# The step and gate-rank columns of a projection: from narrow moving operands to weights in four column groups

## What is computed

```python
z, xbc, dt_raw, q, k, v, g_out, gk_low = jnp.split(h @ p['w_in'], offsets, axis=-1)
gf = jax.nn.log_sigmoid((gk_low @ p['gk_up_f'] + p['gk_bias_f']).astype(f32)) / GLA_GATE_NORM
gb = jax.nn.log_sigmoid((gk_low @ p['gk_up_b'] + p['gk_bias_b']).astype(f32)) / GLA_GATE_NORM
'dt_f': jax.nn.softplus((dt_raw + p['dt_bias_f']).astype(f32)),
'dt_b': jax.nn.softplus((dt_raw + p['dt_bias_b']).astype(f32)),
```

## Time and profile before

| what | value |
|---|---|
| median of three runs | 2600.0 us |
| time of the profiled execution | 2598.53 us |
| its span, first to last instruction | 2596.5 us |
| TensorE busy over the span | 2285.3 us (88%) |
| mean granted TensorE clock over the span | 0.913 of 2.4 GHz |
| span from the first feature product to the last step's small products | 64.17 to 666.31 us |
| TensorE busy in it | 587.5 of 602.14 us, granted clock 0.90 |
| VectorE, ScalarE busy in it | 199.3 us, 129.4 us |

### The profile page before, as it was taken

The page is one execution under the profiler, slowest core; times in us unless marked ns, Lnnn a source line. Parts: engine busy times, 40 slices in busy tenths (PEclk is TensorE's granted clock), DMA queues, the critical chain, the costliest instruction groups (busy, mean ns, idle before and its releaser), DMA issues. The chain is left out here.

```text
span 2596.5 us, 37174 instructions
## 1 busy us (share of the span) xinstructions
PE 2285.3 (88%) x12243; PEld 1813.3 (70%) x12243; DVE 1604.0 (62%) x2000; ACT 1136.2 (44%) x1469; POOL 565.7 (22%) x535
## 2 busy tenths in 40 slices
PE   3999999999689997599999804999999999999990
PEld 1777777766467776588888703887778787878770
DVE  1233333323353443777777353999999999999993
ACT  0122221222255553223233103777777777777772
POOL 1000000000000000144344143333333333333332
PEclk7988898988889998599999857999999999999995
DMA  7123322332276664588787261647897868989967
GB/s 278 58 95 108 108 77 94 108 108 92 101 267 232 237 243 170 196 289 262 253 271 234 65 222 43 201 126 230 281 318 238 293 213 285 351 259 347 340 226 275
DMA packets 207806, 531.79 MB, mean 205 GB/s; under 512 B 14624, under 2 KB 47803, under 8 KB 204635
## 3 DMA queue, kind: packets, MB, share of 16 engines
q1 hardware_dynamic: 180587, 434.68, 46.4%
q0 software_dynamic: 23664, 83.18, 13.1%
q10 hardware_dynamic: 3456, 12.58, 1.3%
HBM read 400.77 MB, written 129.62 MB: 204 GB/s over the span
## 5 line engine op out<-in xcount | busy, mean ns | idle before, releaser
L547 PE MATMUL pf<-hT,w_in_sb 128*128 128x256 f32 x1440 | 331.5, 395 | 1.1 <-DVE hT L628 1.1
L547 PEld LDWEIGHTS pf<-hT,w_in_sb 128*128 128x128 f32 x1440 | 286.5, 200 | 43.5 <-DVE hT L628 1.5
L2019 ACT ACTIVATE w_hi_e<-w_gates 128x2048 fp32r (+1 forms) x103 | 197.5, 1919 | 234.4 <-issue 103.4
L2145 DVE TENSOR_TENSOR w_lo_e<-w_gates,w_hi_e 128x2048 fp32r<-128x2048 f32 x103 | 236.3, 2295 | 33.4 <-ACT w_hi_e L2019 33.4
L2145 DVE TENSOR_TENSOR w_lo_e<-w_ups,w_hi_e 128x2048 fp32r<-128x2048 f32 x102 | 233.5, 2289 | 36.0 <-ACT w_hi_e L2019 35.9
L2145 DVE TENSOR_TENSOR w_lo_e<-w_downs,w_hi_e 128x2048 fp32r<-128x2048 f32 x100 | 228.3, 2283 | 0.0
L2019 ACT ACTIVATE w_hi_e<-w_ups 128x2048 fp32r (+1 forms) x102 | 195.2, 1913 | 26.3 <-PE pd_e L2092 24.6
L2019 ACT ACTIVATE w_hi_e<-w_downs 128x2048 fp32r x100 | 191.1, 1911 | 0.9
L2092 PE MATMUL pg_e<-w_hi_e,x_hi_e 128*128 128x512 f32 x408 | 167.1, 410 | 7.1 <-DVE w_lo_e L2145 7.1
L1997 POOL DMA_INDIRECT x_mid<-yb_e,to_e x50 | 126.9, 2538 | 190.7 <-DVE yb_e L2189 188.7
L2092 PE MATMUL pd_e<-w_hi_e,h_hi_e 128*128 128x512 f32 x400 | 162.1, 405 | 0.0
(11 more groups left out here) (363 smaller groups left out, 4669.1 us busy)
## 6 DMA issues: line engine op xcount, KB each, us to landing
w_gates<-in_w_gate_dram SPq DMA_DIRECT2D x32, 2048.0 KB, 11.6
w_ups<-in_w_up_dram SPq DMA_DIRECT2D x32, 2048.0 KB
w_downs<-in_w_down_dram SPq DMA_DIRECT2D x32, 2048.0 KB
tok_rec<-tm SPq DMA_DIRECT2D x9, 1936.0 KB, 7.2
rec_s<-tok_rec SPq DMA_DIRECT2D x18, 968.0 KB, 6.0
w_mod_half<-in_w_mod_dram SPq DMA_DIRECT2D x16, 1024.0 KB, 6.4
abc_m<-a_rows SPq DMA_DIRECT2D x16, 1024.0 KB, 4.9
qk_rec<-qk_s SPq DMA_DIRECT2D x16, 768.0 KB, 3.2
```

The source lines that it names most:

```text
L547: mm = pe.matmul(pf[n % 2][:, f, :], w[:, k, c0:c0 + P], h[:, k, :], start=(k == 0), stop=(k == KT - 1))
L2019: act.activation(w_hi[:, s % 3:s % 3 + 1, :], raw(part, half, place), ACT.Copy).then_inc(hi_done, 1)
L2145: dve.tensor_tensor(w_lo[:, s % 3:s % 3 + 1, :], raw(part, half, place), w_hi[:, s % 3:s % 3 + 1, :].bitcast(F32), ALU.subtract).then_inc( ...
```

## The change

The step and gate-rank columns become the weights: `w_small` holds 8 step columns, 16 gate-rank columns and 8 columns of zeros, and the eight products of a step go to four groups of 32 partitions of `psm` in turn (feature tiles 0 and 4 to the first, and so on), with all 256 tokens as the moving operand. What comes out is already in feature order, in four partial sums. VectorE copies it once to `quarters` [128 x 256] and adds column 24 of the identity, which makes row 24 a row of ones. The gate product takes `quarters` as weights against a `gk_up` matrix of 128 rows that has the 16 rows of the gates in each of the four groups and the biases in row 24, so that the product adds up the four partial sums. The steps come by two products against `sel_dt` (128 x 16), and VectorE copies these to `small_sb`. The two transposes and the two bias products are gone. The loads of the small matrices are 12 where they were 6.

```diff
-            sp.dma_start(w_small[:, :, 16:32], ...[:, :, O_GK:]).then_inc(w_in_loaded, 16)
+            sp.dma_start(w_small[:, :, SH:SH + RANK], ...[:, :, O_GK:]).then_inc(w_in_loaded, 16)
...
-        small_sb = sb("small_sb", [P, 2, 32])
-        gkT = sb("gkT", [RANK + 1, 2, P])
-        up = sb("gk_up", [RANK + 1, 2 * GQK])
-        dtb = sb("dt_bias", [1, 2 * SH])
+        small_sb = sb("small_sb", [P, 2, 2 * SH])
+        quarters = sb("quarters", [P, GRP])
+        up, sel_dt = sb("gk_up", [P, 2 * GQK]), sb("sel_dt", [P, 2 * SH])
...
+            sp.wait_ge(const_done, 3)
+            for d, n in enumerate(("f", "b")):
+                for j in range(4):
+                    sp.dma_start(up[32 * j + SH:32 * j + SH + RANK, GQK * d:GQK * (d + 1)], A[f"gk_up_{n}"][0]).then_inc(small_loaded, 16)
+                sp.dma_start(up[ONE:ONE + 1, GQK * d:GQK * (d + 1)], A[f"gk_bias_{n}"]).then_inc(small_loaded, 16)
+            sp.wait_ge(wsm_done, 3)
+            for d, n in enumerate(("f", "b")):
+                sp.dma_start(sel_dt[ONE:ONE + 1, SH * d:SH * (d + 1)], A[f"dt_bias_{n}"]).then_inc(small_loaded, 16)
...
+                    act.wait_ge(dt_done, it + 1)
+                    act.activation(soft[s][:, 512:528], small_sb[:, s, :], ACT.Abs).then_inc(abs_done, 1)
...
-            pool.memset(gkT[:, :, :], 1.0).then_inc(const_done, 1)
-            pool.wait_ge(const_done, 2)
+            pool.memset(up[:, :], 0.0).then_inc(const_done, 1)
+            pool.memset(w_small[:, :, ONE:32], 0.0).then_inc(const_done, 1)
+            pool.wait_ge(const_done, 3)
...
-                for s in range(2):
-                    for k in range(KT):
-                        pe.matmul(psm[:, s * 32:s * 32 + 32], h[:, k, s * P:(s + 1) * P], w_small[:, k, :],
-                                  start=(k == 0), stop=False)
-                    mm = pe.matmul(psm[:, s * 32:s * 32 + 16], C["ones"][0:1, :], dtb[0:1, :], start=False, stop=True)
+                for k in range(KT):
+                    j = k % 4
+                    mm = pe.matmul(psm[32 * j:32 * j + 32, 0:GRP], w_small[:, k, :], h[:, k, :], start=(k < 4), stop=(k >= 4))
                 mm.then_inc(small_ps, 1)
...
+                if is_ctx:
+                    pe.wait_ge(small_loaded, 16 * 12)
                 for s in range(2):
-                    mm = pe.transpose(psm[0:RANK, 128 + s * P:256 + s * P], small_sb[:, s, 16:32], ident[:, :])
-                mm.then_inc(gk_ps, 1)
-                pe.wait_ge(gk_done, it + 1)
+                    mm = pe.matmul(psm[:, GRP + 2 * SH * s:GRP + 2 * SH * (s + 1)], quarters[:, s * P:(s + 1) * P], sel_dt[:, :], start=True, stop=True)
+                mm.then_inc(dt_ps, 1)
                 pe.wait_ge(tok_done, it * 2 + 2)
                 for s in range(2):
-                    pe.matmul(pz[s][:, :], gkT[:, s, :], up[:, :], start=True, stop=True).then_inc(g_ps, 1)
+                    pe.matmul(pz[s][:, :], quarters[:, s * P:(s + 1) * P], up[:, :], start=True, stop=True).then_inc(g_ps, 1)
...
+            for d in range(2):
+                dve.tensor_reduce(sel_dt[:, SH * d:SH * (d + 1)], ident[:, :].rearrange("p (j c) -> p c j", j=4)[:, 0:SH, :], AX,
+                                  ALU.add).then_inc(wsm_done, 1)
...
-                dve.tensor_copy(small_sb[:, :, :], psm[:, 0:64].rearrange("p (s c) -> p s c", s=2)).then_inc(small_done, 1)
+                dve.tensor_scalar(quarters[:, :], psm[:, 0:GRP], ident[:, ONE:ONE + 1], None, ALU.add).then_inc(small_done, 1)
...
-                dve.wait_ge(gk_ps, it + 1)
-                dve.tensor_copy(gkT[0:RANK, :, :], psm[0:RANK, 128:384].rearrange("p (s c) -> p s c", s=2)).then_inc(gk_done, 1)
+                dve.wait_ge(dt_ps, it + 1)
+                dve.tensor_copy(small_sb[:, :, :], psm[:, GRP:GRP + 4 * SH].rearrange("p (s c) -> p s c", s=2)).then_inc(dt_done, 1)
```

More of the change, by code:

```diff
@@ L261, in _ @@
                 sp.dma_start(w_in_sb[:, k, :], A["w_in"][0][k * P:(k + 1) * P, O_XBC:O_G]).then_inc(w_in_loaded, 16)
-            sp.dma_start(w_small[:, :, 16:32], A["w_in"][0].rearrange("(k p) c -> p k c", p=P)[:, :, O_GK:]).then_inc(w_in_loaded, 16)
+            sp.dma_start(w_small[:, :, SH:SH + RANK], A["w_in"][0].rearrange("(k p) c -> p k c", p=P)[:, :, O_GK:]).then_inc(w_in_loaded, 16)
         @block.gpsimd
@@ L320, in projection @@
     NF = 10
+    ONE = SH + RANK
     col = [i * P for i in range(6)] + [o - O_XBC for o in (O_Q, O_Q + P, O_K, O_K + P)]
@@ L359, in projection @@
         tok_ps, tok_done = sem("tok_product"), sem("tok_done")
-        small_ps, small_done, gk_ps, gk_done, g_ps, abs_done, exp_done, ln_done, min_done, g_done = (
-            sem(n) for n in ("small_product", "small_copied", "gk_transposed", "gk_copied", "g_product",
+        small_ps, small_done, dt_ps, dt_done, g_ps, abs_done, exp_done, ln_done, min_done, g_done = (
+            sem(n) for n in ("small_product", "quarters_copied", "dt_product", "dt_copied", "g_product",
                              "abs_done", "exp_done", "ln_done", "min_done", "g_done"))
@@ L472, in body @@
                     act.activation(soft[s][:, 0:512], pz[s][:, :], ACT.Abs).then_inc(abs_done, 1)
-                    act.activation(soft[s][:, 512:528], small_sb[:, s, 0:16], ACT.Abs).then_inc(abs_done, 1)
+                    act.wait_ge(dt_done, it + 1)
+                    act.activation(soft[s][:, 512:528], small_sb[:, s, :], ACT.Abs).then_inc(abs_done, 1)
                 for s in range(2):
@@ L510, in _ @@
         def _(pe):
-            pe.wait_ge(wsm_done, 2)
-            pe.wait_ge(const_done, 2)
-            pe.wait_ge(small_loaded, 16 * 6)
+            pe.wait_ge(wsm_done, 3)
+            pe.wait_ge(const_done, 3)
             def turned(it, use, buf, is_ctx, rounds):
@@ L611, in _ @@
             dve.wait_ge(w_loaded, 16 * KT + 16)
-            for j in range(2):
-                dve.tensor_copy(w_small[:, :, 8 * j:8 * j + 8], w[:, :, O_DT - O_XBC:O_DT - O_XBC + 8]).then_inc(wsm_done, 1)
-            dve.wait_ge(small_loaded, 16 * 6)
+            dve.tensor_copy(w_small[:, :, 0:SH], w[:, :, O_DT - O_XBC:O_DT - O_XBC + SH]).then_inc(wsm_done, 1)
+            for d in range(2):
+                dve.tensor_reduce(sel_dt[:, SH * d:SH * (d + 1)], ident[:, :].rearrange("p (j c) -> p c j", j=4)[:, 0:SH, :], AX,
+                                  ALU.add).then_inc(wsm_done, 1)
             def head(it, use, buf, is_ctx):
@@ L667, in body @@
                     dve.tensor_copy(line[:, :], macc[:, :]).then_inc(line_done, 1)
-                dve.wait_ge(gk_ps, it + 1)
-                dve.tensor_copy(gkT[0:RANK, :, :], psm[0:RANK, 128:384].rearrange("p (s c) -> p s c", s=2)).then_inc(gk_done, 1)
+                dve.wait_ge(dt_ps, it + 1)
+                if not is_ctx:
+                    dve.wait_ge(abs_done, it * 4)
+                    dve.wait_ge(min_done, it * 4)
+                dve.tensor_copy(small_sb[:, :, :], psm[:, GRP:GRP + 4 * SH].rearrange("p (s c) -> p s c", s=2)).then_inc(dt_done, 1)
+                dve.wait_ge(dt_done, it + 1)
                 t = tm[buf]
@@ L678, in body @@
                     dve.tensor_scalar(t[:, s, T_GF:T_GF + 512], pz[s][:, :], 0.0, 1 / 16.0, ALU.min, ALU.mult).then_inc(min_done, 1)
-                    dve.tensor_scalar(t[:, s, T_DT:T_DT + 16], small_sb[:, s, 0:16], 0.0, None, ALU.max).then_inc(min_done, 1)
+                    dve.tensor_scalar(t[:, s, T_DT:T_DT + 16], small_sb[:, s, :], 0.0, None, ALU.max).then_inc(min_done, 1)
                 for s in range(2):
```

11 lines of the change are left out of this document (2 added, 9 removed).

## The result

The changed kernel takes 2517.3 us (median of four, 2513.3 to 2519.7) against 2600.2 (four, 2599.6 to 2601.1): a ratio of 0.968, 95% interval 0.9666 to 0.9695. The forecast was 2521 us. The profiled execution took 2518.98 us with a span of 2517.0 us.

A forecast was written before the change was run, and what follows sets the result against it. TensorE's path alone, partly at low clock, was taken to bound the projection's nine steps. Terms summed to 78.7 us off the profiled 2598.5, giving 2519.8; with 1.5 for the median, 2521 us, range 2508 to 2548.

The forecast's parts named there:

- A: Small products of each step: in four column groups they take 1.0 us instead of 4.34; 30.1 us saved.
- B: Value products behind the small products: the low clock there all goes; 24.6 us saved.
- C: Ahead of the transposes of the next x: a new TensorE wait of 0.45 us in eight steps; 3.6 us lost.
- D: Ahead of the gate product: two products replace transposes, copy and wait, the gate product's own time unchanged; 9.0 us saved.
- E: End of the step and the features after it: of 34 us lost to low clock, 19 go and 15 stay.
- F: Start of the kernel: GpSimd clears larger buffers ahead of the context's load; 0.4 us lost.
- Rival 1: End of the step: the clock still falls in every step, 19 us not gained, 2540 us; chance 0.17.
- Rival 2: Small products: column groups don't hide weight loads (2543 us) or the clock still falls behind them (2546 us); chance 0.11.
- rival 4: Features: the clock once fallen stays at half, 2793 us if throughout; chance 0.02 together with everything else slower.
- Rival 3: End of the step and features: the clock never falls, the other 15 us go too, 2506 us; chance 0.07.
- Rival 5: Whole step: another engine holds it and the gain doesn't reach the end; some us, no chance of its own.

The follow-up runs named there:

- The filler: Kernel before, with three useless 128x256 products between the gate-rank transposes and TensorE's wait ahead of the gate product; 2583.0 us, ratio 0.9930.

## Why the prediction was right, term by term

From the two traces, over all steps; the stretch as a whole is 625.4 - 541.4 = 84.0 us shorter. The mechanisms of A, B, C and D are as forecast and their sizes within 1.1 us; E has the right sign and place, and the wrong size.

- A, forecast 30.1: 9 x 4.34 - (8 x 0.98 + 1.00) = 30.2, and 8 x 0.12 = 1.0 more as the next products start 0.88 us after the half slab instead of 1.00.
- B, forecast 24.6: 23.8. The low clock behind the small products is gone in all steps; the first half of the values then takes 6.97 us and not 6.87.
- C, forecast -3.6: -3.9. The wait is there in seven steps and not in eight, 7.52 - 6.97 = 0.55 us each; the context's step has none. The transposes behind the wait take 0.93 us instead of 0.88, another 0.4.
- D, forecast 9.0: 8 x (1.55 - 0.46) + (0.94 - 0.85) = 8.8. In the last step TensorE waits for ScalarE's copy of the values instead.
- E, forecast 19: 24.4. From the gate product to the features 59.0 us became 46.4 over eight steps (12.6), the features of these steps 294.4 became 282.6 (11.8). This was the term that I had mis-sized, twice over. Features at full clock take 34.7 us, not 34.05: the 141 records in 30 us include those that stand over the edges of the stretch (three stretches of 10 us have 48 each, 144 together), so an instruction is 34.71 / 160 = 0.217 us and not 0.213. With 46.3 us as the least for the eight ends, 12.7 + 16.7 = 29.4 us were to be had and not 34. And what stayed is 5.0 us, not 15. The step of the prediction that failed is the sentence by which the new stretch, as long as the last step's small products, would still fall in some steps, a little later than before. Over the gate product and the transposes it fell in none; three times it fell at the features' start, once of these 0.1 us earlier, in the turned line.
- The 5.85 us at full clock in E came out well (5.79) by two errors that cancel: seven transposes take 0.84 us where I counted 0.76, and the turned line takes 0.82 where I had 0.93 (scaled like those transposes it would have been 0.78).
- F, forecast -0.4: -0.3. The memsets took 0.52 and 0.15 us instead of 0.30, and the first feature product starts that much later against the first memset.
- The rest: the span is 79.5 us shorter, so 4.5 of the 84.0 aren't in it. Of these 2.0 us lie ahead of the first feature product, and apart from the 0.3 of F they lie ahead of GpSimd's first memset of the projection (40.31 and 41.97), which the change doesn't touch; 2.5 lie behind the projection, in instructions that are the same. Both are of the size by which these stretches differ from profile to profile (the first feature product 64.2 to 67.4 us, the rest behind the projection 1905.4 to 1910.8 us, over the kernels with the same stages there).

The terms A to E add up to 84.3 us; the first features are 0.2 us shorter and C's transposes take 0.4 more, which leaves the 84.0 within rounding. Forecast for A to E were 79.1. That the spans differ by 79.5, so near to the 78.7 of the sum, is therefore luck in part: E was 5.4 us too small, and the stretches that the change doesn't touch took 4.2 us longer in this profile. The medians differ by 82.9.

Rival 1 had the rule of the Trainium skill for it (TensorE: Matmul & The Clock Gate, Part 4) that transposes don't count as busy like products. The trace shows that it doesn't decide here: the fourteen transposes run at 1.00 in all eight steps (0.93 and 1.01 us for seven transposes, up to 1.76 before). Rival 2 is out by 0.98 us and the clock behind it, rival 4 by the features. Rival 3, a clock that never falls, is out by the three falls, but it was the nearer of the two neighbours in E: 5.0 us of low clock stayed. Rival 5 showed nothing beyond the waits in C and D.

Why E came out better is what the runs on rows and waits settle. From the gate product to the features either is enough to keep the clock: full rows with the wait (no fall in eight steps), 17 rows without the wait (one fall). With neither it falls (in all eight steps with 32 rows and the wait, 6.3 us from the gate product to the features in one of them, 7.2 to 7.4 in the others). They aren't worth the same: the rows alone also leave full features in eight steps of eight, the missing wait in two. The change does both at once. I had named both in the prediction, but as two weak reasons against rival 1, and D has the 128 rows as without effect, which is true of the product's own time only. The other reason that I gave, that nothing fell behind the last step's small products, doesn't hold, as the same products in two other runs show.

What stays open: the changed kernel has full features in five of eight steps, but with the wait put back, which makes the stretch longer, it has seven, and costs 4 us more where 8 were forecast. Which steps fall isn't settled by the program: counting the context as step 0, the low clock is in the features of steps 1, 5 and 6 in one profile of the changed kernel and of 3, 7 and 8 in the other. The filler's picture alternates, so that what went before may play a part, but with one or two profiles of each I can't tell a rule from chance.

## What to carry to other kernels

In a stage that TensorE bounds, read the granted clock stretch by stretch and price each sparse stretch with what runs slowly behind it: here narrow products of 4.3 us cost up to 3.4 us in themselves and the values after them, and a 1.2 us wait with a 17-row product 3.7 us on average (29.4 over eight steps) in the transposes and features after it. Make the long operand the moving one and the narrow one the weights, let partial sums be added by the next product instead of by a turn and a copy, and fill a small product's rows with zeros where that costs no time. Then look which wait is late next, on the other engines too: moving two copies of VectorE forward was worth another 9 us.

## What was not expected of the hardware

- How many rows a product fills matters for the clock behind it, even when they add nothing: with 111 more rows that meet zeros the gate product is as long (1.98 us) and the kernel 31 us faster.
- Three useless dense products in a wait of 1.16 us made the kernel 18 us faster.
- Behind 3.55 us of products with 32 weight columns in one column group the clock stays at 1.00 in nine of nine steps; in or behind 4.3 to 5.1 us of full-width products with 32 moving columns it fell in eight of nine, and in the run with 128 rows in nine of nine.
